# Recurrent mixer of a two-block transformer: 1/rms on eviction, gates pair by pair, decay among the experts, two output chunks in whole precision

## The reference

```python
h = rms_norm(x, norm_mix_g[1])
gate, xr = jnp.split(h @ w_in, [D_RNN], axis=-1)      # 1024 -> 2 x 1024
gate = jax.nn.gelu(gate)
xr = causal_conv(xr, conv_w) + conv_b                   # four taps
r = sigmoid(xh @ w_a + b_a)                             # 8 heads of 128
i = sigmoid(xh @ w_x + b_x)
log_a = 8 * r * log_sigmoid(lam)
a = exp(log_a)
b = sqrt(-expm1(2 * log_a)) * (i * xr)
hseq = scan(h_t = a_t * h_{t-1} + b_t)
x = x + (gate * hseq) @ w_out                           # 1024 -> 1024
```

## Time and profile before

| | us |
|---|---|
| median of 3 runs (2249.54 to 2251.11) | 2251.02 |
| the profiled execution, its own time | 2254.54 |
| its span in the profile | 2252.7 |
| TensorE busy | 1922.7 (85%) |
| VectorE busy | 949.7 (42%) |
| ScalarE busy | 653.0 (29%) |
| mean granted clock | 0.947 |

### The profile page before, as it was taken

One profiled execution on the slowest core, in us unless ns is written; L12 is line 12 of the kernel. 1 busy time (PEld: TensorE's weight loads), 2 busy tenths in 40 slices (PEclk: granted clock), 3 DMA queues, 4 the chain that ended last, 5 costly groups with the idle time before them and its releaser, 6 DMA issues.

```text
span 2252.7 us, 35555 instructions
## 1 busy us (share of the span) xinstructions
PE 1922.7 (85%) x16018; PEld 1596.7 (71%) x16022; DVE 949.7 (42%) x1317; ACT 653.0 (29%) x912; POOL 67.0 (3%) x64
## 2 busy tenths in 40 slices
PE   7887776677679867667769999999999999999999
PEld 7863333333478433333439999999999999999999
DVE  4721111111484111111137556756556556666555
ACT  4410000000363000000024445435445444434443
POOL 0000000000000000000000001200000000200000
PEclk9899989989897998998989999999999999999999
DMA  9379999999845999999985554445554554435551
GB/s 382 119 311 426 428 427 427 427 427 427 358 150 217 428 427 428 427 427 427 427 366 179 183 177 167 148 169 171 185 187 169 187 184 155 167 130 191 185 187 57
DMA packets 65278, 622.93 MB, mean 277 GB/s; under 512 B 10848, under 2 KB 11360, under 8 KB 14432
## 3 DMA queue, kind: packets, MB, share of 16 engines
q1 hardware_dynamic: 65120, 620.58, 69.8%
HBM read 619.50 MB, written 1.05 MB: 275 GB/s over the span
## 4 chain that ended last, share of the span: by engine, by line
PE 62%; DMA 22%; DVE 11%; ACT 3%; issue 1%; SPq 1%; DVEq 0%; ACTq 0%
PE ps L451 14%; PE ps L452 14%; PE ps L453 14%; DMA expert_ring_a<-in_moe_w_down 6%; PE ps L663 6%; DMA expert_ring_b<-in_moe_w_down 6%; DMA dense_ring<-in_moe_w_down 6%; PE ps L651 5%; DVE w_lo L1318 3%; PE ps L640 3%; PE ps L900 2%; PE ps L674 2%; DMA expert_ring_a<-in_moe_w_up 2%; DMA dense_ring<-in_dense 2%; ACT w_hi L949 1%
## 5 line engine op out<-in xcount | busy, mean ns | idle before, releaser
L451 PE MATMUL ps<-h_hi,w_hi 128*128 128x256 f32 x2112 | 607.3, 288 | 35.2 <-DVE h_lo L1324 10.9
L1318 DVE TENSOR_TENSOR w_lo<-dense_ring,w_hi 128x1024 fp32r<-128x1024 f32 x384 | 473.5, 1251 | 351.0 <-ACT w_hi L949 350.6
L452 PE MATMUL ps<-h_lo,w_hi 128*128 128x256 f32 x2112 | 602.9, 285 | 0.0
L453 PE MATMUL ps<-h_hi,w_lo 128*128 128x256 f32 x2112 | 602.5, 285 | 0.0
L949 ACT CAST w_hi<-dense_ring 128x1024 fp32r<-128x1024 f32 x384 | 394.5, 1045 | 298.3 <-PE ps L453 284.9
L451 PEld LDWEIGHTS ps<-h_hi,w_hi 128*128 128x128 f32 x2112 | 410.3, 194 | 41.1 <-issue 20.2
L452 PEld LDWEIGHTS ps<-h_lo,w_hi 128*128 128x128 f32 x2112 | 410.7, 194 | 0.1
L453 PEld LDWEIGHTS ps<-h_hi,w_lo 128*128 128x128 f32 x2112 | 410.8, 194 | 0.0
L1587 DVE TENSOR_TENSOR work<-work,ps 128x256 f32<-128x256 f32 x32 | 13.5, 421 | 530.8 <-ACT work L1135 530.8
L451 PE MATMUL ps<-hid_hi,w_hi 128*128 128x256 f32 x704 | 199.7, 284 | 0.6 <-DVE w_lo L1318 0.6
L452 PE MATMUL ps<-hid_lo,w_hi 128*128 128x256 f32 x704 | 199.2, 283 | 0.0
(11 more groups left out here) (277 smaller groups left out, 2065.8 us busy)
## 6 DMA issues: line engine op xcount, KB each, us to landing
dense_ring<-in_dense SPq DMA_DIRECT2D x204, 1024.0 KB, 4.8
expert_ring_a<-in_moe_w_gate SPq DMA_DIRECT2D x24, 2048.0 KB, 31.2
dense_ring<-in_moe_w_up SPq DMA_DIRECT2D x24, 2048.0 KB, 30.7
dense_ring<-in_moe_w_down SPq DMA_DIRECT2D x20, 2048.0 KB, 31.9
expert_ring_b<-in_moe_w_gate SPq DMA_DIRECT2D x20, 2048.0 KB, 31.8
expert_ring_b<-in_moe_w_up SPq DMA_DIRECT2D x20, 2048.0 KB, 34.3
expert_ring_a<-in_moe_w_down SPq DMA_DIRECT2D x20, 2048.0 KB, 33.8
dense_ring<-in_moe_w_gate SPq DMA_DIRECT2D x20, 2048.0 KB, 30.9
```

Source lines behind the costliest of these rows:

```text
L451: mm(o, w[0], x[0], start=start, stop=False, **kw)
L452: mm(o, w[0], x[1], start=False, stop=False, **kw)
L453: return mm(o, w[1], x[0], start=False, stop=stop, **kw)
L1318: V.tensor_tensor(half_of(key, f, 1), tile_of(slot(key), key, f), half_of(key, f, 0).bitcast(F32), ALU.subtract).then_inc(remainder.up(key ...
```

## The change

What it does: 
- The mixer takes x times gain as the feed forwards do (`gained`, `less`); the squares' sum is VectorE's, and 1/rms comes in when xr (`scaled_input`) and the gate branch (`scaled_gate`) leave PSUM, which VectorE now does.
- The first tap of the convolution is ScalarE's, with Identity, scale and bias.
- The gates are multiplied and followed through pair by pair between the chunks; the square of the decay is ScalarE's.
- Lambda's first two operations are at the entry, its Exp in the first expert layer, the rest of `decay` after VectorE's quad 1 there.
- Output chunks 8 and 9 are not split: they multiply gate x scan as it lies, in float32.
- The squares for the next expert layer lie 2048 columns further on in the work area.

The diff, cut: where much goes, the lines taken out are left out, since they stand in the kernel before.

```diff
@@ -111,7 +111,7 @@
-    chunks += [(("lru", 8 + c), cols("c_w_out", 0, c * CHUNK), True) for c in range(4)]
+    chunks += [(("lru", 8 + c), cols("c_w_out", 0, c * CHUNK), c >= 2) for c in range(4)]
@@ -305,7 +305,7 @@
-    squares_of_moe = view(work, 0, KD)
+    squares_of_moe = view(work, 2048, KD)
@@ -320,6 +320,9 @@
+    AS_LOADED = [key for key, _, split in chunks if key in [("lru", 8 + c) for c in range(4)] and not split]
@@ -464,7 +467,7 @@
-            PE.wait_ge(pooled, "ss", s)
+            PE.wait_ge(vec if s == "lru" else pooled, "ss", s)
@@ -505,7 +508,10 @@
-                tile_products((s, first + j), 1 + j, ready, x, ks=ks)
+                if (s, first + j) in AS_LOADED:
+                    as_loaded((s, first + j), 1 + j, lambda k: (vec, "gy", k // 2), lru_gate)
+                else:
+                    tile_products((s, first + j), 1 + j, ready, x, ks=ks)
@@ -584,29 +590,43 @@
+            def gates(g):
...
+                    claim(2 + m, acted, "tanh", g, m)
...
+                        ins = mm(bank[2 + m][:, f * T:(f + 1) * T], (wa, wx)[m][:, h, :], lru_xr[:, h, :], start=True, stop=True)
...
+            for j, b in enumerate((0, 1, 2, 0)):
+                claim(b, vec, "xr_in", j)
+                tile_products(("lru", j), b, h_of("lru"))
+                if j == 1:
+                    square_mean("lru", 3)
+            for n in ("c_w_a", "c_w_x"):
+                PE.wait_ge(dense_loaded[place_of["lru", n]], "lru", n)
+            for j in range(4):
+                if j < 2:
+                    gates(j)
+                elif j == 2:
+                    gates(2)
+                    gates(3)
+                claim(4 + j, vec, "scaled_gate", j)
...
+        def as_loaded(key, b, ready, x):
...
+            w = k_view(slot(key), CHUNK)
+            PE.wait_ge(dense_loaded[place_of[key]], *key)
+            for f in range(2):
+                for k in range(KD):
+                    PE.wait_ge(*ready(k))
+                    ins = mm(bank[b][:, f * T:(f + 1) * T], w[:, k, f * P:(f + 1) * P], x[:, k, :], start=k == 0, stop=k == KD - 1)
+                ins.then_inc(products.up(key, f), 1)
@@ -974,7 +994,9 @@
-            if s == "f10":
+            if s == "lru":
+                ACT.wait_ge(products, *last_of(0, "b", 2))
+            elif s == "f10":
@@ -984,7 +1006,7 @@
-            if s == "f10":
+            if s in hT_free:
@@ -1051,27 +1073,33 @@
+                gained("lru", q)
...
+            table(ACTF.Sqrt)
+            squares("lru")
+            hi(("lru", 2))
+            rms_later("lru", 3)
+            hi(("lru", 3))
...
+            def first_tap(j):
+                ACT.wait_ge(vec, "xr_in", j)
+                for c in (2 * j, 2 * j + 1):
+                    ins = S.activation(lru_xr[:, c, :], lru_pad[:, c, 0:T], ACTF.Identity, bias=small_of("c_conv_b", c, 1),
+                                       scale=small_of("c_conv_w", c, 1))
+                ins.then_inc(acted.up("tap", j), 1)
...
+            def gates(g):
+                for m in range(2):
+                    ACT.wait_ge(products, "gate", g, m)
+                    ACT.wait_ge(vec, "half_b")
+                    for f in range(2):
+                        h = 2 * g + f
+                        ins = S.activation((lru_ra, lru_bx)[m][:, h, :], bank[2 + m][:, f * T:(f + 1) * T],
+                                           ACTF.Tanh, bias=lru_cst[:, 4 + m, h:h + 1], scale=0.5)
+                    ins.then_inc(acted.up("tanh", g, m), 1)
+                ACT.wait_ge(acted, "tanh", g, 0)
@@ -1079,32 +1107,32 @@
+                ACT.wait_ge(acted, "ra", g)
+                ACT.wait_ge(vec, "input", g)
+                S.activation(pair(lru_xr, g), pair(lru_ra, g), ACTF.Square).then_inc(acted.up("ra_squared", g), 1)
...
+            first_tap(0)
+            hi(("lru", 4))
+            first_tap(1)
+            hi(("lru", 5))
+            first_tap(2)
+            gates(0)
+            first_tap(3)
+            gates(1)
+            hi(("lru", 6))
+            gates(2)
+            gates(3)
+            hi(("lru", 7))
...
+            for j in range(4):
+                ACT.wait_ge(vec, "scaled_gate", j)
+                S.activation(pair(lru_gate, j), pair(lru_gate, j), ACTF.Gelu_apprx_tanh).then_inc(acted.up("gelu", j), 1)
@@ -1124,6 +1152,9 @@
+            if l == 0:
+                ACT.wait_ge(vec, "lam")
+                S.activation(lru_cst[:, 1, :], lru_cst[:, 2, :], ACTF.Exp).then_inc(acted.up("lam"), 1)
@@ -1381,6 +1412,7 @@
+            lambdas()
@@ -1438,12 +1470,16 @@
+        def lambdas():
...
+            lam, s = small_of("c_lambda"), lru_cst[:, 2, :]
+            seq(V.tensor_scalar(s, lam, -1.0, None, ALU.mult))
+            seq(V.tensor_tensor(s, s, lam, ALU.min), "lam")
...
-            seq(V.tensor_scalar(s, lam, -1.0, None, ALU.mult))
-            seq(V.tensor_tensor(s, s, lam, ALU.min), "lam")
@@ -1463,45 +1499,88 @@
+            for q in range(4):
+                less("lru", q)
...
+            DVE.wait_ge(acted, "sq", "lru", 1)
+            seq(V.tensor_tensor(square_sum, hflat[:, 0:2 * T], hflat[:, 2 * T:4 * T], ALU.add))
+            for q in (2, 3):
+                DVE.wait_ge(acted, "sq", "lru", q)
+                seq(V.tensor_tensor(square_sum, square_sum, hflat[:, 2 * q * T:2 * (q + 1) * T], ALU.add),
+                    *(("ss", "lru") if q == 3 else ()))
+            lo(("lru", 2))
...
+            reciprocal_later("lru")
...
+            def scaled_input(j):
+                DVE.wait_ge(products, ("lru", j), 1)
+                seq(V.tensor_tensor(lru_pad[:, 2 * j:2 * j + 2, PAD_C:], two(bank[(0, 1, 2, 0)[j]]), over_tiles(rinv), ALU.mult),
+                    "xr_in", j)
...
+            def convolve(j):
+                DVE.wait_ge(acted, "tap", j)
+                for tap in (1, 2, 3):
+                    for c in (2 * j, 2 * j + 1):
+                        if tap > 1:
+                            DVE.wait_ge(vec, "conv", tap - 1, c)
+                        V.scalar_tensor_tensor(lru_xr[:, c, :], lru_pad[:, c, tap:tap + T], small_of("c_conv_w", tap * KD + c, 1),
+                                               lru_xr[:, c, :], ALU.mult, ALU.add).then_inc(
+                                                   vec.up(*(("xr", c) if tap == 3 else ("conv", tap, c))), 1)
...
+                DVE.wait_ge(vec, "xr", 2 * g + 1)
+                V.scalar_tensor_tensor(pair(lru_bx, g), pair(lru_bx, g), 1.0, pair(lru_xr, g), ALU.add, ALU.mult).then_inc(
+                    vec.up("input", g), 1)
...
+            def more_factors(g):
+                DVE.wait_ge(acted, "ra_squared", g)
+                V.scalar_tensor_tensor(pair(hT, g), pair(lru_xr, g), 1.0, pair(hT, g), ALU.add, ALU.mult).then_inc(
+                    vec.up("factor", g), 1)
...
+            def scaled_gate(j):
+                DVE.wait_ge(products, ("lru", 4 + j), 1)
+                V.tensor_tensor(pair(lru_gate, j), two(bank[4 + j]), over_tiles(rinv), ALU.mult).then_inc(
+                    vec.up("scaled_gate", j), 1)
...
+            scaled_input(0)
+            lo(("lru", 3))
+            convolve(0)
+            scaled_input(1)
+            lo(("lru", 4))
+            convolve(1)
+            scaled_input(2)
+            lo(("lru", 5))
+            convolve(2)
+            factors(0)
+            scaled_input(3)
+            more_factors(0)
+            convolve(3)
+            factors(1)
+            lo(("lru", 6))
+            scaled_gate(0)
+            more_factors(1)
+            factors(2)
+            factors(3)
+            scaled_gate(1)
+            more_factors(2)
+            lo(("lru", 7))
+            more_factors(3)
...
+                DVE.wait_ge(vec, "input", g)
...
+                if g > 1:
+                    scaled_gate(g)
...
+                DVE.wait_ge(vec, "scan", 2 * g + 1)
...
+            for g in range(4):
@@ -1568,6 +1647,8 @@
+                if l == 0 and qd == 1:
+                    decay()
@@ -1923,7 +2004,7 @@
-            q = [work[:, i * 2 * T:(i + 1) * 2 * T] for i in range(3)]
+            q = [work[:, 2048 + i * 2 * T:2048 + (i + 1) * 2 * T] for i in range(3)]
@@ -1949,6 +2030,8 @@
+                elif old in AS_LOADED:
+                    SP.wait_ge(products, old, 1)
@@ -2048,7 +2131,8 @@
-                    SP.wait_ge(remainder, [k for k in order[:last] if place_of[k] == d][-1], 1)
+                    old = [k for k in order[:last] if place_of[k] == d][-1]
+                    SP.wait_ge(products if old in AS_LOADED else remainder, old, 1)
```

More of the change, by code:

```diff
@@ L1053, in lru @@
             for q in range(4):
-                square("lru", q)
-            rms("lru")
+                gained("lru", q)
             hi(("lru", 1))
-            y, t = lru_cst[:, 1, :], lru_cst[:, 2, :]
-            ACT.wait_ge(vec, "lam")
-            S.activation(y, t, ACTF.Exp).then_inc(acted.up("lam"), 1)
-            for j in range(4):
-                hi(("lru", 2 + j))
```

(43 more changed lines are left out.)

29 lines of the change are left out of this document (removed).

## The result

The changed kernel takes 2238.68 us (median of 6 runs, 2236.92 to 2244.29); the kernel before, timed beside it, 2250.82 (6 runs, 2248.76 to 2253.40). The ratio is 0.995 (95% interval 0.994 to 0.996): 12.1 us less, where 13.0 were forecast. The profiled execution of the changed kernel took 2236.98 us (span 2235.2).

A forecast was written before the change was run, and what follows sets the result against it. Expert layers were taken as bound by DMA, the mixer by a chain of waits through all engines. Hand-laid steps gave 13.4 us less, taken as 13.0 for hand-overs: 2238.0 in runs, range 2231 to 2246.

The forecast's parts named there:

- x done: Mark where the first expert layer's last addition is done and the mixer begins; 591.0 us in the kernel before.
- E: End of the mixer's last chunk, 11, which lets SP issue loads; forecast at 689.8 against 703.2, 13.4 us less.
- The start: Mixer's front: with the norm gone, chunk 0 starts at 593.1 to 594.5, taken as 594.3; before, 7 us later.
- The tail: Mixer after chunk 7: chunk 8 starts at 660.9, half clock until 665, chunk 8 ends 669.8, chunk 9 676.7.
- 18.4 us from 679.3 to 660.9: Mixer's output products: chunk 8 reads the first pair unsplit at 660.9 instead of 679.3, called the largest single gain.
- The middle: Mixer from the mean to chunk 7: TensorE waits some 3 us before gates 0, 2.4 before chunk 7, ending 655.1.
- Decay among the experts: First expert layer: 6 us of small VectorE operations hidden by 17 us of queued transfers, cost 0; uncovered, 6 more.
- Table loads: ScalarE in the mixer: Tanh and Exp share one load, then square root and gelu; 1.28 us each, no drain.
- next: Mark where SP issues the next pieces after the mixer, at 726.38 before; forecast to stay 23.2 us behind E.
- whatever moves chunk 11's product moves the rest: Mixer's end: the rest of the program moves by as much, if the 23.2 us to 726.38 stay.
- The gain wasn't eaten: Rival, 14%: half clock through chunks 8 and 9 (up to 11.8 more) or ScalarE 3 later; gain 5 to 8.
- The stream does hang on E: Against a 7% rival: experts' loads released by something else, mixer's gain becomes idle DMA queue, nothing arrives; 2250.
- A clock that falls in the middle: Rival, 4%: pauses at the mixer's gates bring 1.2 GHz, 5.75 more per chunk, four cost 23; 2261.

The follow-up runs named there:

- bank7: Changed kernel with chunk 2 in bank 7 instead of bank 2, so the gates of pair 0 don't wait for pair 2's eviction; 2233.8 us.
- norm_front: Changed kernel with squares, means, root, reciprocal and normed copies in front of the mixer's chunk 0 again, plain copies at the evictions; 2241.5 us.
- warm: Changed kernel with 22 products of zeros filling TensorE's pause between chunks 7 and 8; 2235.7 us.
- tail: Changed kernel with chunks 8 and 9 multiplied in turn, one half of the outputs first, each gated product right behind its scan; 2236.5 us.
- decay_30: Changed kernel with 150 more small VectorE operations (30 us) behind the decay in the first expert layer; 2258.8 us.
- decay_12: Changed kernel with 60 more small VectorE operations (12 us) behind the decay in the first expert layer; 2239.3 us.
- tail_by_pair: Changed kernel with chunks 8 and 9 multiplied pair by pair of input tiles for all outputs, each gated product right after its scan; 2229.3 us.

## Why the prediction was right, step by step

Times from x done, forecast against profile. Forecast: 591.0 is zero. "Ends" of chunk 7 leave out the last 0.16 us, in which its last product runs out.

| step | forecast | measured |
|---|---|---|
| chunk 0 starts | 3.3 | 1.8 |
| reciprocal done | 20.2 | 18.2 |
| gates 0 wait for pair 2's eviction, then start | 3 us, 31.9 | 2.5 us, 29.8 |
| wait before chunk 7 | 2.4 us | 2.3 us |
| chunk 7 ends | 64.1 | 62.7 |
| idle before chunk 8, start | 5.8 us, 69.9 | 5.2 us, 68.1 |
| chunk 9 ends | 85.7 | 84.7 |
| E | 98.8 | 98.0 |

**The start** was forecast 1.5 late. TensorE's pause after the combination, 2.86 in the kernel before, is there again: 2.53. The floor that the forecast worked out (593.1, or 2.1) was nearly right; the 1.2 on top of it, to 594.3, were not needed. What fills the pause is open: the profile names VectorE's first low half, but that was written at 589.33, 1.3 us before the product started. The forecast stayed 1 to 2 us behind from there to chunk 9, and 0.8 at E: the 0.8 between 13.4 and 14.2.

**The tail**, from chunk 7's end to E, took 35.3 us where 34.7 were forecast: chunk 8 ran at half clock for some 5 us (0.53 and 0.79 in the two stretches from 655 to 665) where 4.1 were assumed. But the sentence that called it the largest gain, "18.4 us from 679.3 to 660.9", set the first product of the new chunk 8 against the last pair's products of the old one. The old chunk 8 began at 673.48; first against first it is 14.4 us from x done (82.5 to 68.1), and 9.6 of that were won by chunk 7's end. Undone this part is worth 3.9 us, done alone 5.0. The forecast for E didn't use the 18.4. One bound of the tail is wrong too: 681.6 as the latest end of chunk 8 "half through both" is neither chunk 8's end (674.7 by the same prices) nor chunk 9's (688.5); the 11.8 of the rival fits the latter.

**The parts**, each by its own run: norm out of the front 6.9, whole-precision chunks 3.9, decay 0.5. Each was undone alone in the kernel after, and read from one profile. The 2.9 that remain of 14.2 (gates pair by pair, first taps and squares on ScalarE) are by subtraction; no run tried them alone.

**The middle** had the right length, and half of the reason. By the forecast's own prices chunk 3 ends at 620.4 (608.9 and two chunks), not at 619, so the wait before the gates is 2.5 and not 3, as measured. "ScalarE is behind here" holds for the wait before chunk 7 (2.2 of it are left in bank7). But ScalarE had itself waited 2.1 us for TensorE's gates, and bank7 shows that the 2.5 us before gates 0 were all on the path.

**Decay among the experts**: 0, as forecast, and the 17 us of cover measure 18. **Table loads**: three from the gates to gelu, as forecast, and no drain after one (0.01 us), as in the earlier trace rows. "ScalarE: Activation LUTs" of the Trainium skill, section "What ACT_TABLE_LOAD costs", adds a drain of 1.38 us to a load. The trace doesn't agree: none is seen after these loads, nor ahead of them (the roots' load starts at 645.36, where the work before it ends at 645.35).

**E to the end**: 23.2 us again, but it is not a constant. Eight kernels have 17 us of half clock behind E, beginning 1 to 2 us after it, while TensorE runs router products of 36 columns and one column, and 23.2 us to next; in the others some of it is missing, and they take 21.0 to 22.4. The start of the second block's feed forward is alike: 7 us of half clock there in the kernel before, none in the kernel after, where that part (1081.4 to 1079.0 us, from the second expert layer's end) is 2.4 us shorter. The kernel after has 3.4 us of half clock ahead of that mark instead, and 446.2 us from next to it against 444.9. The spread of the runs, up to 7 us for one kernel, is of this size, but that it comes from these stretches is argued from one profile each, not shown. For the same reason "whatever moves chunk 11's product moves the rest" is not shown one for one: in norm_front E moved by 6.9 against x done and the time by 2.8.

**The rivals.** The gain wasn't eaten: the clock took 2.6 in the tail (warm). The stream does hang on E. A clock that falls in the middle exists (profiles of tail, norm_front and decay_30), but a stretch of 3.4 us costs TensorE some 1.7, not 5.75 a chunk, and in norm_front the wait before chunk 8 took it up (3.9 us instead of 5.2).

**How near is luck.** 13.4 forecast for E and 14.2 measured is a mechanism that held step by step. That the time came within 0.7 us of the 2238.0 forecast is in part luck: the runs of the kernel after spread over 7.4 us, and the medians differ by 2.1 less than the mixers do in the profiles.

## What to carry to other kernels

Before you count an earlier start as gain, set like against like, the first product against the first. Then ask what the consumer did meanwhile: a product that eats its input pair by pair hides part of the chain that feeds it (here an input that was complete 8.0 us earlier moved the end by 3.9). Order the products so that little is left behind the last input. A wait that "another engine would set anyway" may be the one that sets that engine: give the disputed tile its own bank and see. And where a stream of transfers follows, look how deep it is queued at the place to which you move work.

## What the runs showed of the hardware

- Around x done twelve of fourteen profiles have 3.4 us of half clock, either ahead of it or behind it; tail has 6.8 behind it, decay_12 3.4 on either side. A comparison of stages has to look at both sides of its mark.
- TensorE's pause of 5.2 us brought the 1.2 GHz level from 655, and so did each pause of 3.7 to 10.0 us before chunk 8 in the other profiles; 22 products of zeros in that pause kept the clock at 1.00. Pauses of 2.2 to 3.4 us in the middle were followed by a drop in three of the profiles only (tail, decay_30, norm_front).
- A whole-precision product of 128x256 is two rows of the trace and takes 13.98 / 32 = 0.44 us from start to start at full clock (tail_by_pair); the three products in halves that replace it take 0.36.
- 256 columns of Identity with scale and bias take ScalarE 592 ns, two of them 1.09 us (0.50 from start to start), where 0.41 had been taken from its neighbours.
